# State space heads before the rotation on VectorE, narrow key weights, shorter suffix sums and no meta columns in four stages, in a two-block decoder kernel

## The reference

```
h = rmsnorm(h_res, n_mix_pre);  proj = h @ w_in     # split into 14 parts
y_a = short_conv_mixer(a_b, a_c, a_x, ...)          # b_gate * conv(c_gate * x)
y_b = ssd_mixer(s_z, s_xbc, s_dt, ...)              # 16 state space heads
y_c = retention_mixer(r_q, r_k, r_v, r_g, ...)      # 4 heads, rotated q and k
y_d = stick_breaking_mixer(sb_q, sb_k, sb_v, ...)   # 8 heads
mix = (sum over branches of sigmoid(gate) * (y @ w_branch)) @ w_out
h_res += rmsnorm(mix, n_mix_post);  then a gated FFN in the same manner

# ssd_mixer, per head j of group g (inclusive causal):
y = (C B^T * exp(acs_l - acs_s)) @ (x * dt)  + x * d;   y *= silu(z);   grouped rmsnorm
# retention_mixer, per head:
y = ((rotate(q) rotate(k)^T / 16) * gamma^(l - s)) @ v; normalised;     y *= silu(g)
# stick_breaking_mixer, per head (strictly causal mask m):
l_neg = where(m, log_sigmoid(-z), 0)
log_w = log_sigmoid(z) + reverse_cumsum(l_neg) - l_neg;  y = where(m, exp(log_w), 0) @ v
```

## Time and profile before

| | us |
|---|---|
| median of three runs | 2362.74 |
| lowest, highest | 2362.01, 2369.19 |
| the profiled execution | 2365.18 |
| its span in the trace | 2362.4 |
| stages r_q and r_k, layer 0 and layer 1 | 76.4, 75.0 |
| stages a_b, up_a of layer 1 | 24.2, 45.2 |
| stage b_kq, layer 1 | 69.3 |

### The profile page before, as it was taken

How to read it: one execution, slowest core, us unless ns; L and a number is a source line. 1 busy time by engine, 2 the same in 40 slices (tenths; PEclk the granted TensorE clock), 3 DMA queues, 4 the chain that set the end, 5 groups by cost and what they waited for, 6 DMA issues and landing times.

```text
span 2362.4 us, 40934 instructions
## 1 busy us (share of the span) xinstructions
PE 2221.9 (94%) x17110; PEld 2175.4 (92%) x17110; DVE 1568.9 (66%) x2564; ACT 1173.2 (50%) x1930; POOL 23.4 (1%) x32
## 2 busy tenths in 40 slices
PE   4999997989989998899999899999998999998998
PEld 4889997989989998899999899999997999998998
DVE  6867888676559586665555666486867656566763
ACT  2634445554444566445454644444755454555543
POOL 0000000000000000000000100000000000000000
PEclk8999998999999999999999999999999999999999
DMA  9869995356645553353434455545543535344553
GB/s 348 290 222 275 351 374 204 113 190 213 203 156 175 174 185 127 126 160 126 161 117 143 152 172 168 170 161 182 194 145 116 166 120 170 125 143 152 188 179 117
DMA packets 123142, 428.19 MB, mean 181 GB/s; under 512 B 14480, under 2 KB 18768, under 8 KB 122320
## 3 DMA queue, kind: packets, MB, share of 16 engines
q1 hardware_dynamic: 122960, 425.58, 53.9%
HBM read 422.87 MB, written 2.66 MB: 180 GB/s over the span
## 4 chain that ended last, share of the span: by engine, by line
PE 81%; DVE 9%; ACT 4%; DMA 4%; issue 1%; SPq 0%; DVEq 0%; ACTq 0%
PE stream L491 24%; PE stream L493 23%; PE stream L492 23%; PE stream L497 5%; DVE w_lo L391 2%; DMA raw<-in_ffn_up 2%; PE side L630 2%; PE side L623 1%; ACT w_hi L862 1%; DMA raw<-in_ffn_down 1%; DVE mod_raw L1339 1%; DVE mod_raw_first L1339 1%; ACT L1039 1%; DVE scratch L1727 1%; DMA mod_raw_first<-in_mod_w 0%
## 5 line engine op out<-in xcount | busy, mean ns | idle before, releaser
L491 PE MATMUL stream<-h_hi,w_hi 128*128 128x272 f32 (+2 forms) x3408 | 990.6, 291 | 30.9 <-DVE x_res L1399 11.6
L493 PE MATMUL stream<-h_hi,w_lo 128*128 128x272 f32 (+2 forms) x3408 | 978.4, 287 | 0.0
L492 PE MATMUL stream<-h_lo,w_hi 128*128 128x272 f32 (+2 forms) x3408 | 976.5, 287 | 0.0
L391 DVE TENSOR_TENSOR w_lo<-raw,w_hi 128x1024 fp32r<-128x1024 f32 (+1 forms) x650 | 781.0, 1207 | 173.4 <-ACT w_hi L862 171.4
L862 ACT CAST w_hi<-raw 128x1024 fp32r<-128x1024 f32 (+1 forms) x650 | 662.6, 1034 | 288.3 <-DMA raw<-in_ffn_down 103.6
L491 PEld LDWEIGHTS stream<-h_hi,w_hi 128*128 128x128 f32 x3408 | 647.0, 190 | 36.7 <-issue 29.7
L492 PEld LDWEIGHTS stream<-h_lo,w_hi 128*128 128x128 f32 x3408 | 646.2, 190 | 0.7
L493 PEld LDWEIGHTS stream<-h_hi,w_lo 128*128 128x128 f32 x3408 | 646.8, 190 | 0.0
L491 PE MATMUL stream<-f_hi,w_hi 128*128 128x256 f32 (+1 forms) x704 | 199.8, 284 | 4.8 <-issue 2.6
L493 PE MATMUL stream<-f_hi,w_lo 128*128 128x256 f32 (+1 forms) x704 | 199.3, 283 | 0.0
L492 PE MATMUL stream<-f_lo,w_hi 128*128 128x256 f32 (+1 forms) x704 | 198.8, 282 | 0.0
(11 more groups left out here) (323 smaller groups left out, 2906.2 us busy)
## 6 DMA issues: line engine op xcount, KB each, us to landing
raw<-in_ffn_up SPq DMA_DIRECT2D x176, 512.0 KB, 3.6
mod_raw<-in_mod_w SPq DMA_DIRECT2D x96, 512.0 KB, 5.8
raw<-in_ffn_down SPq DMA_DIRECT2D x64, 512.0 KB, 3.6
raw<-in_a_cx SPq DMA_DIRECT2D x32, 512.0 KB, 3.7
raw<-in_up_a SPq DMA_DIRECT2D x32, 512.0 KB, 3.6
raw<-in_up_b SPq DMA_DIRECT2D x32, 512.0 KB, 3.5
raw<-in_up_c SPq DMA_DIRECT2D x32, 512.0 KB, 3.5
raw<-in_b_kq SPq DMA_DIRECT2D x32, 512.0 KB, 3.4
```

The costliest lines, as they stand in the source:

```text
L391: eng.tensor_tensor(w_lo[:, x.slot, 0:x.kb * P], raw[:, x.slot, 0:x.kb * P], w_hi[:, x.slot, 0:x.kb * P].bitcast(F32), ALU.subtract).then_ ...
L491: pe.matmul(ps, w_hi[:, x.slot, W], rhs[0][:, k, off:off + n], start=first, stop=False)
L492: pe.matmul(ps, w_hi[:, x.slot, W], rhs[1][:, k, off:off + n], start=False, stop=False)
L493: return pe.matmul(ps, w_lo[:, x.slot, W], rhs[0][:, k, off:off + n], start=False, stop=last)
```

## The change

1. On VectorE, `head(c)` comes before tile c in r_q and r_k, instead of after it (new argument `ahead` of `run`).
2. `packed_scores` uses only as many key columns as exist, 16 in the third segment, and writes 16 partitions there. The zeroed tails of `r_k` and `b_k` go, and `b_k` has pitch 272 instead of 384. For the state space groups VectorE clears the third segment's columns in each side bank (`clear`), and the group scores wait for that (`rows_clear`) instead of for `x_scaled`.
3. The suffix sums are three products: one of 432 columns with `suffix`, one of 144 with ones, one of 16 columns repeated by broadcast into two places with ones.
4. In layer 1 stages a_b, s_z, r_q and r_g have 256 columns. Three clears set the meta columns of `s_z`, `r_q` and `r_g` to zero.

```diff
-  Phase(f"a_b{l}", "conv_gate", 8, l=l),        # the same for s_z, r_q, r_g
+  Phase(f"a_b{l}", "conv_gate", 8, l=l, **tail),
...
-            def packed_scores(b, key, kt, q, qt, tiles=1, pitch=TOK):
+            def packed_scores(b, key, kt, q, qt, tiles=1):
                 for n, (c, q0, w) in enumerate(SEG):
+                    m = KEYS[n][1]
                     for i in range(tiles):
-                        at = pitch * (kt + i) + n * P
-                        last = pe.matmul(b[:, c:c + w], key[:, at:at + P], ...
+                        at = TOK * (kt + i) + n * P
+                        last = pe.matmul(b[0:m, c:c + w], key[:, at:at + m], ...
...
-                    pe.wait_ge(side["x_scaled"], 6 * l + (4, 4, 5, 6)[g])
+                    pe.wait_ge(side["rows_clear"], 4 * l + g + 1)
...
-                    pe.matmul(b[:, 0:272], suffix, S[:, 0:272], start=True, stop=False)
+                    pe.matmul(b[:, 0:PACK], suffix, S[:, 0:PACK], start=True, stop=False)
                     pe.matmul(b[:, P:272], ONES[:, :], S[:, 272:416], start=False, stop=False)
-                    pe.matmul(b[:, 256:272], ONES[:, :], S[:, 416:432], start=False, stop=True)
-                    pe.matmul(b[:, 272:416], suffix, S[:, 272:416], start=True, stop=False)
-                    pe.matmul(b[:, 400:416], ONES[:, :], S[:, 416:432], start=False, stop=True)
-                    pe.matmul(b[:, 416:432], suffix, S[:, 416:432], start=True, stop=True)\
+                    both = b[:, P:416].rearrange("p (a n) -> p a n", a=2)[:, :, P:]
+                    pe.matmul(both, ONES[:, :], S[:, 416:432].unsqueeze(1).to_broadcast([P, 2, 16]), start=False, stop=True)\
                         .then_inc(side["sb_r"], 1)
...
-            def run(name, beside=None):
+            def run(name, beside=None, ahead=None):
                 p = by[name]
                 for x, mods in zip(p.seq, p.mod_tiles):
+                    if ahead is not None:
+                        ahead(x.t)
                     tile(p, x, mods)
...
+                    if m >= 3:
+                        dve.wait_ge(side["x_scaled"], 6 * l + m + 1)
+                        clear(m - 2)
+
+                def clear(b):
+                    dve.memset(B[b][:, SEG[2][0]:PACK], 0.0).then_inc(side["rows_clear"], 1)
...
-                run(f"r_q{l}", beside=lambda c: head(c))
-                run(f"r_k{l}", beside=lambda c: head(8 + c))
+                run(f"r_q{l}", ahead=lambda c: head(c))
+                run(f"r_k{l}", ahead=lambda c: head(8 + c))
...
-                dve.memset(RK[:, 8 * TOK:], 0.0)
...
-                dve.memset(BK[:, :].rearrange("p (a n) -> p a n", a=8)[:, :, TOK:], 0.0)
```

More of the change, by code:

```diff
@@ L135, in plan @@
         tail = seq if l else {}
-        ph += [Phase(f"a_cx{l}", "cx", 16, l=l, lead=4, raw=16, raw_of=f"pre{l}", raw_rhs="RB"), Phase(f"a_b{l}", "conv_gate", 8, l=l),
+        ph += [Phase(f"a_cx{l}", "cx", 16, l=l, lead=4, raw=16, raw_of=f"pre{l}", raw_rhs="RB"), Phase(f"a_b{l}", "conv_gate", 8, l=l, **tail),
                Phase(f"up_a{l}", "merge", 16, "HY", l=l, **tail),
                Phase(f"dt{l}", "dt", 1, l=l), Phase(f"s_x{l}", "conv_silu", 8, l=l),
-               Phase(f"s_bc{l}", "conv_silu", 8, l=l, t0=8), Phase(f"s_z{l}", "act", 8, l=l),
-               Phase(f"r_q{l}", "rotate", 8, l=l), Phase(f"r_k{l}", "rotate", 8, l=l),
+               Phase(f"s_bc{l}", "conv_silu", 8, l=l, t0=8), Phase(f"s_z{l}", "act", 8, l=l, **tail),
+               Phase(f"r_q{l}", "rotate", 8, l=l, **tail), Phase(f"r_k{l}", "rotate", 8, l=l),
                Phase(f"up_b{l}", "merge", 16, "HB", l=l, **tail),
-               Phase(f"r_v{l}", "vtok", 8, l=l), Phase(f"r_g{l}", "act", 8, l=l),
+               Phase(f"r_v{l}", "vtok", 8, l=l), Phase(f"r_g{l}", "act", 8, l=l, **tail),
                Phase(f"up_c{l}", "merge", 16, "HY", l=l, **tail),
@@ L202, in flat @@
     if len(buf.shape) == 2:
-        pitch = 384 if buf.shape[1] == 8 * 384 else TOK
-        at = t * pitch + off
+        at = t * TOK + off
         return buf[:, at:at + n]
@@ L299, in two_layer_pair @@
         RSQ, RRT = tiles("r_squares", [P, 8, TOK], 43.2), tiles("r_roots", [P, 4, TOK], 39.2)
-        RQ, RK = tiles("r_q", [P, 8 * TOK], 51.3), tiles("r_k", [P, 8 * TOK + P - 16], 59.3)
+        RQ, RK = tiles("r_q", [P, 8 * TOK], 51.3), tiles("r_k", [P, 8 * TOK], 59.3)
         RV, RG, RP = tiles("r_v", [P, 3, D], 16), tiles("r_g", [P, 8, TOK], 28), tiles("r_p", [P, 2, PACK], 36)
-        BK, BV, BQ = tiles("b_k", [P, 8 * 384], 16), tiles("b_v", [P, 3, D], 28), tiles("b_q", [P, 8 * TOK], 40)
+        BK, BV, BQ = tiles("b_k", [P, 8 * TOK], 16), tiles("b_v", [P, 3, D], 28), tiles("b_q", [P, 8 * TOK], 40)
         ZS, SA, SS, SW = (tiles(n, [P, 2, PACK], 48 + 4 * i) for i, n in enumerate(("b_z", "b_a", "b_s", "b_w")))
@@ L613, in attention @@
                     inside={2: lambda: head(7), 3: lambda: head(8), 4: lambda: head(9), 5: lambda: head(10)})
-            def packed_scores(b, key, kt, q, qt, tiles=1, pitch=TOK):
+            def packed_scores(b, key, kt, q, qt, tiles=1):
                 for n, (c, q0, w) in enumerate(SEG):
+                    m = KEYS[n][1]
                     for i in range(tiles):
-                        at = pitch * (kt + i) + n * P
-                        last = pe.matmul(b[:, c:c + w], key[:, at:at + P], q[:, TOK * (qt + i) + q0:TOK * (qt + i) + q0 + w],
+                        at = TOK * (kt + i) + n * P
+                        last = pe.matmul(b[0:m, c:c + w], key[:, at:at + m], q[:, TOK * (qt + i) + q0:TOK * (qt + i) + q0 + w],
                                          start=i == 0, stop=i == tiles - 1)
@@ L933, in tile @@
                         dst, func, scale = acts[p.name]
-                    off = p.off if dst is M else 0
+                    off = p.off if dst is M or dst is Z or dst is RG else 0
                     if p.norm:
@@ L1708, in front @@
                         take_steps()
+                        clear(0)
                     elif i < 4:
```

30 lines of the change are left out of this document (18 added, 12 removed).

## The result

| | before | after |
|---|---|---|
| median, us | 2364.68 (4 runs, 2362.01 to 2369.19) | 2324.49 (4 runs, 2323.56 to 2325.87) |
| ratio, 95% interval | | 0.9829 [0.9811, 0.9847] |
| the profiled execution's span | 2362.4 | 2321.9 |

40.2 us less, where the prediction said 44.6; its forecast of 2318.1 is missed by 6.4 us, and its range of 2311 to 2329 holds.

A forecast was written before the change was run, and what follows sets the result against it. The prediction took TensorE's list of products plus its holes as the bound. Savings of 27.2 + 7.0 + 4.2 + 6.2 = 44.6 us from the median of 2362.7 gave 2318.1 us, range 2311 to 2329.

The forecast's parts named there:

- Heads ahead of the rotation: r_q and r_k: VectorE's head work before the rotation removes TensorE's holes, one per layer in up_b too; 27.2 us saved.
- The walk through chunk 13: r_k of layer 1: head product 13 has 2.7 us to spare; banks released 4.8 us after the chunk.
- The rule that decided it: r_q and r_k: TensorE stops if VectorE releases a bank pair later than two chunks, 7.9 us, after the chunk.
- VectorE becomes the bound: r_k: VectorE has 33.1 us of work against TensorE's 32.4; half the holes return, 8 us less saved, 2326; chance 0.12.
- The slower-than-before rival: r_q and r_k, odd chunks: rotation behind the heads holds the banks past 7.9 us; 2384 us; chance 0.02.
- Suffix sums: Stick breaking heads: three products take 1.18 us instead of 1.62, 0.44 x 16 heads, 7.0 us saved.
- No meta columns: a_b, s_z, r_q, r_g of layer 1: 256 instead of 272 columns, 1.55 a stage, 6.2 us saved.
- 16-column key weights: Packed scores: narrow loads save 2.2 us in 24 one-tile heads and 2.1 in retention, 4.2 after rounding.
- its worst end: Key weights in the packed scores: 0 saved if a narrow load takes as long as a wide one.
- The clears: VectorE's four clears of 16 PSUM columns per layer before the masks: at worst 3.6 us in all, taken as 0.
- the high end: Whole kernel, 2329 us: VectorE-bound (8 us) with part of the 3.6 for the clears.
- The low end: Whole kernel: 44.6 + 2.6 + 3.6 us saved, 2312, rounded down to 2311.

The follow-up runs named there:

- the loaded kernel: The changed kernel with one needless VectorE sum over 432 columns more in each of a layer's 16 state space heads; 2333.9 us.
- wide keys: The changed kernel with full 128-column key weights, zero tails, pitch 384 and no clears; 2320.93 us, ratio 0.983.
- the second: The changed kernel itself measured once more, beside two versions built on it; 2324.53 us, ratio 0.9837.

## Why the prediction was right or wrong

**Heads ahead of the rotation: 27.2 forecast, 27.0 measured** by the kernel with this edit alone. The two stages came out at 63.7 (forecast 63 to 64), 62.2 in layer 1 (62). The walk through chunk 13 was right in kind and a little short in size: the banks come free 5.6 us after the chunk instead of 4.8. The rule that decided it, two chunks or 7.9 us, leaves 2.3 us. VectorE as a whole had 2.9 us (layer 1) to 5.7 (layer 0) of room, as the loaded kernel shows. The rival "VectorE becomes the bound" named the right engine and the right stage, and missed by those 3 us. The slower-than-before rival would have needed the release at 7.9; in after it comes at 5.6 at the latest. In the loaded kernel it comes at 8.1, and TensorE still doesn't stop for it, so 7.9 was no fixed bound: what delays VectorE's head steps delays TensorE as well.

**Suffix sums: 7.0 forecast, 6.5 measured.** By the kernel with this edit alone they take 1.19 us a head, where 1.18 was forecast: the three products together were priced right. That saves 0.43 in seven heads of a layer. Of the missing 0.5, 0.3 are the eighth: in the kernel before its sums took 1.53, not 1.62, and with three products 1.15 (layer 0) and 1.33 (layer 1), so it gives 0.38 and 0.20.

**No meta columns: 6.2 forecast, 6.1 measured**: a_b 1.51, s_z 1.61, r_q 1.49, r_g 1.46 (layer 0 against layer 1; s_z and r_g with wide keys), and a_b without a hole, at 22.7 where 22.6 was forecast. The rule of the Trainium skill that was weighed there (page TensorE: Matmul & The Clock Gate, section Back-to-back issue gap) would have given 1.6; the trace sides with the rows of up_a, 8 ns for 16 columns.

**16-column key weights: 4.2 saved forecast, 2.1 to 2.3 lost.** This is the term that failed, in sign. It read the spacing of 0.11 between full loads as a price of loading 128 columns, and gave a narrow load its share of it; its worst end was 0, "if a narrow load takes as long as a wide one". But a full load costs little that shows as long as it runs beside the product ahead of it: 0.05 us a head more than one of 66 columns. A 16-column load among full ones loses that cover: 0.09 us before the narrow pass, 0.02 more debt behind it, and nothing saved from the narrow pass to the next product (0.14 us in both). With two tiles a head, four narrow loads stand in a row, and there the sum is a gain of 0.06 instead of the 0.26 expected. The end of the range below nothing, which no row excluded, was left out. The clears, priced at 0 to 3.6 us, cost nothing that shows: s_z lost 0.45 us in four groups, 0.11 each, and a stick breaking head, which has no clear, lost as much.

The Trainium skill (same page, section LDWEIGHTS) has load time go with the columns at 1.2 a ns, which would have made the term 7.5. The runs agree with the slope where the load is pulled ahead: from 128 to 66 columns a group is 0.05 us shorter, 0.8 ns a column. They disagree with it below: from 64 to 16 columns a group gets 0.08 us shorter, 1.6 ns a column, and all of these groups are longer than with 128. The same page, section The mechanism, has a load pulled ahead when it goes to other rows of the array or to the background buffer; here the rows are the same throughout, and it is the number of columns that decides. Which buffer a load goes to, no trace here shows.

**The rest.** up_c of layer 1 became 1.6 us longer, which no term had. In that stage too TensorE waits 2.2 us for a sigmoid, in after and in before; in after a spell at the lower clock follows (granted 0.50), in before none (1.00 in the whole stage):

```profile
1908.50:1911.90 3.40, 3.40 (x18) 3.40 (x17) 2.28 (x2) 3.18 (x5) 0.00 (x0) 0.50 0.03 7
...
1931.70:1980.80 49.10, 46.89 (x390) 46.33 (x389) 30.13 (x46) 28.79 (x43) 0.00 (x0) 1.00 0.52 172
```

All kernels with the 256-column stages show it (50.60 to 50.66 us), all without them don't (49.08 to 49.10), until the sigmoids came earlier. Why this hole tips the clock and that one doesn't is open: no run varied it alone. Adding up: 27.0 + 6.5 + 6.1 - 2.1 - 1.6 = 35.9, and the stages behind the unchanged blocks give 36.4. The medians differ by 40.2 in the first comparison and by 38.4 in the second; the 2 to 4 us over the sum are within the scatter of the unchanged blocks. From 2362.7 the sum of 36 gives 2326.8, still inside the range. That is partly luck: the high end was made for VectorE as the bound and for the clears, neither of which came, and covered the key weights and the new spell instead. The low end adds 3.6 us saved that the prediction derives nowhere as a saving; two spells of 1.4 would be 2.8, and the end 2312.7.

## What to carry to other kernels

Ask of an operation made smaller whether it was on the path at all: a weight load that is pulled ahead is nearly free, and a smaller one that isn't pulled ahead costs more. Where single narrow weights stand among full ones, measure them widened above 64 columns, or put them side by side. When an engine in order serves two customers, put first the work whose operands are already there, and compare what is held back with the depth of the buffers; here that was worth 27 us, at an engine that was busy for two thirds of the time.

## What the hardware showed that was not expected

- A weight load of 16, 32 or 64 columns behind a product with full weights starts about 0.22 us after the second 144-column pass did; loads of 66 to 128 columns start with it. A score group takes 1.04, 1.06, 1.12 us with 16, 32, 64 columns and 0.87, 0.89, 0.91, 0.93 with 66, 80, 112, 128.
- Loads and passes of 16 columns in a row run 0.025 us apart.
- An operand repeated by a broadcast costs nothing of its own: 0.14 us for the pair of L755, as before for a pair of 16 columns.
- A hole of 2.2 to 2.8 us in the product stream can be followed by a spell at 1.2 GHz that costs 1.5 us; whether one comes varies between kernels that do the same there (up_b of layer 0: 54.16 in after, 52.61 with wide keys).
